# The final normalisation of an attention layer: scale and shift vectors in PSUM banks, epsilon on VectorE, a 512-column first centring piece

## The chip, the cores and the metric

One Trainium2 chip, one core. The metric is the device time of one execution in microseconds (us). The kernel before was timed in three runs. Engines are called as the profile calls them: PE is TensorE, DVE VectorE, ACT ScalarE, POOL GpSimd, and SP the engine whose queue issues most DMAs.

## The reference

One decoder layer on 512 rows of 2048 columns, float32 throughout: a differential attention with eight heads (each with two query and key parts of 128 columns and a value of 256), its output gated by silu(z), projected out and added to the scaled input; then a layer normalisation. What the change touches is the last line:

```
proj = x @ w_in                                   # q | k | v | z, 2048 x 8192
a    = softmax(q1 k1^T * s + bias) - lam * softmax(q2 k2^T * s + bias)
o    = rms_norm(a @ v, subln_g) * (1 - lam_init)
y    = (o * silu(z)) @ w_out                      # 2048 x 2048
r    = 2 ** 0.25 * x + y
out  = (r - mean(r)) * rsqrt(var(r) + 1e-5) * ln_g + ln_b
```

## The kernel before, in words

Each engine has its own program, written out by hand, and the engines meet at semaphores. Every float32 product is made of three fast ones: ACT rounds a weight or activation block to a high part, DVE subtracts that for a low part, and PE multiplies high by high, high by low and low by high.

The eight head pairs go through PE one after another (16 weight quarters each), then the out projection runs in four chunks of 512 columns (`c`), each over eight weight blocks (`i`). Chunks 0 and 2 are summed in the four PSUM banks `proj`, chunks 1 and 3 in the four banks `att`; bank `s` holds row tile `s` of 128 rows. Chunks 0 to 2 go through all four row tiles for each weight block. Chunk 3 goes tile by tile (PE's last loop, L931 to L939): tile `s` is finished with its 48 matmuls, and `tile_done` tells DVE, while PE goes on with the next. The banks `proj` are free from the moment that DVE has read chunk 2 (r_ready 12), and bank `s` of `att` from the moment that DVE has read tile `s` of chunk 3.

For tile `s` of chunk 3, the work is this.

- DVE adds the residual (L724: x_res times alpha, from SBUF, plus the PSUM bank), takes the statistics of 512 columns (L727) and aggregates those of all four chunks into mean and variance (L754).
- POOL adds epsilon to the variance (L379) and raises it to the power -1/2 (L382), which gives `r_std`.
- DVE centres the first 1024 columns, (r - mean) * ln_g, in one instruction (L759), waits for `r_std`, makes shift = -mean * r_std (L763), centres the next 512 columns (L759), then scales by `r_std` and adds ln_b on both pieces (L768). `VECTOR_PIECES` (L951) lists the two.
- ACT normalises the last 512 columns as r * r_std + shift (L541), and POOL multiplies them by ln_g (L387) and adds ln_b (L389). `POOL_PIECE` (L952) is that slice.
- SP stores the three pieces in the order in which they are written here (L328 twice, L330), each when it is ready, and waits at the end for all stores.

ln_g and ln_b lie as 128 x 2048 rows in SBUF, in `scratch` (L108), loaded during chunk 1 (L323, L324). `big` holds the rows r (`r_rows`). ACT's last other work before this stage is the weight splits of chunk 3 (L527), made ahead during chunk 2, and the load of the residual's input (`load_res`, L253, issued on ACT's queue).

Of the kernel before, what the change touches and what calls it, by code (L numbers as in the profile page):

```python
# [33 lines left out]
ALU = mybir.AluOpType  # L34
ACT = mybir.ActivationFunctionType
# [5 lines left out]
D = 2048  # L41
# [3 lines left out]
ST = SEQ // P  # L45
# [10 lines left out]
NC = 512  # L56
CHUNKS = D // NC
# [8 lines left out]
EPS = 1e-5  # L66
# [4 lines left out]
def diff_layer(nc, x, rel_bias, w_in, lam_q1, lam_k1, lam_q2, lam_k2, subln_g, w_out, ln_g, ln_b,  # L71
               x_cols, out):
    with ExitStack() as ctx:  # L73
# [3 lines left out]
        def sem(name):  # L77
            return ctx.enter_context(nc.semaphore(name))
# [29 lines left out]
        ln_g_all, ln_b_all = scratch[:, 0:D], scratch[:, D:2 * D]  # L108
# [22 lines left out]
        mean_var = sb("mean_var", [P, ST, 2])  # L131
        var_eps = sb("var_eps", [P, ST])
# [9 lines left out]
        turned = att[:, 2]  # L142
        av = att[:, 3, 0:PW]

        x_loaded = [sem(f"x_loaded{i}") for i in range(len(X_UNITS))]
        raw_loaded = [sem(f"raw_loaded{i}") for i in range(RING)]
        small_loaded = sem("small_loaded")
# [6 lines left out]
        ln_loaded = sem("ln_loaded")  # L154
# [51 lines left out]
        pool_scaled = sem("pool_scaled")  # L206
        pool_rows_ready = sem("pool_rows_ready")
        centred = sem("centred")
        rows_ready = sem("rows_ready")

        TOTAL = PAIRS * QUARTERS
# [39 lines left out]
        def load_res(eng, c):  # L251

            eng.dma_start(x_res[:], x[0, :, c * NC:(c + 1) * NC].rearrange("(s p) d -> p s d", p=P)  # L253
                          ).then_inc(res_loaded, 16)
# [80 lines left out]
        @block.gpsimd  # L335
        def _(pool):
            nc.gpsimd.memset(ident[:], 0.0).then_inc(ident_zero, 1)
            pool.wait_ge(ident_zero, 1)
            nc.gpsimd.affine_select(out=ident[:], in_=ident[:], compare_op=ALU.not_equal, fill=1.0, base=0,
                                    pattern=[[-1, P]], channel_multiplier=1).then_inc(consts_ready, 1)  # L340
            nc.gpsimd.memset(minus_half[:], -0.5).then_inc(consts_ready, 1)

            def spread_bias(p):

                heads = slice(2 * p, 2 * p + 2)
                pool.dma_start(bias_dram.ap()[heads].rearrange("h q w -> q h w"),
                               line_dram.ap()[heads].unsqueeze(0).to_broadcast([P, 2, BIAS_W])).then_inc(bias_spread, 16)

            nc.gpsimd.memset(bias_line[:, SEQ:BIAS_W], MASKED).then_inc(bias_line_ready, 1)
            pool.wait_ge(table_loaded, 16)  # L350
            for bucket, cols in BUCKET_RUNS:
                nc.gpsimd.tensor_copy(bias_line[:, cols],
                                      table[:, bucket:bucket + 1].to_broadcast([16, cols.stop - cols.start])
                                      ).then_inc(bias_line_ready, 1)
            pool.wait_ge(bias_line_ready, len(BUCKET_RUNS) + 1)
            pool.dma_start(line_dram.ap(), bias_line).then_inc(line_stored, 16)
            pool.wait_ge(line_stored, 16)
            spread_bias(0)
            pool.wait_ge(consts_ready, 2)
            for p in range(PAIRS):  # L360
                pool.wait_ge(bias_spread, 16 * (p + 1))
                if p:
                    pool.wait_ge(max_ready, 2 * ST * p)

                pool.dma_start(bias[:], bass.AP(bias_dram, 2 * p * P * BIAS_W + P - 1,
                                                [[BIAS_W - 1, P], [P * BIAS_W, 2], [1, SEQ]])).then_inc(bias_loaded, 16)
                if p + 1 < PAIRS:
                    spread_bias(p + 1)
                for t in range(ST):
                    n = ST * p + t + 1  # L370
                    pool.wait_ge(sq_ready, n)
                    nc.gpsimd.tensor_scalar(mean_sq[:, t:t + 1], sq_sum[:, t:t + 1], 1.0 / PW, EPS,  # L372
                                            ALU.mult, ALU.add).then_inc(mean_ready, 1)
                    pool.wait_ge(mean_ready, n)
                    nc.gpsimd.tensor_tensor(rms[:, t:t + 1], mean_sq[:, t:t + 1], minus_half[:],  # L375
                                            ALU.pow).then_inc(rms_ready, 1)
            for s in range(ST):
                pool.wait_ge(mv_ready, s + 1)
                nc.gpsimd.tensor_scalar(var_eps[:, s:s + 1], mean_var[:, s, 1:2], 1.0, EPS,  # L379
                                        ALU.mult, ALU.add).then_inc(var_ready, 1)  # L380
                pool.wait_ge(var_ready, s + 1)
                nc.gpsimd.tensor_tensor(r_std[:, s:s + 1], var_eps[:, s:s + 1], minus_half[:],  # L382
                                        ALU.pow).then_inc(r_std_ready, 1)

                part = r_rows[:, s, POOL_PIECE]
                pool.wait_ge(act_normed, s + 1)
                nc.gpsimd.tensor_tensor(part, part, ln_g_all[:, POOL_PIECE], ALU.mult).then_inc(pool_scaled, 1)  # L387
                pool.wait_ge(pool_scaled, s + 1)
                nc.gpsimd.tensor_tensor(part, part, ln_b_all[:, POOL_PIECE], ALU.add).then_inc(pool_rows_ready, 1)  # L389
# [3 lines left out]
        def _(act):  # L393
# [123 lines left out]
            for c in range(CHUNKS):  # L517
                for i in range(OQ):
                    if c == 0 and i in G_STEPS:
                        g_split_hi(G_STEPS[i])  # L520
                    for n in out_splits(c, i):
                        act.wait_ge(raw_loaded[ring(n)], 16 * (n // RING + 1))
                        if n < LAST:
                            act.wait_ge(quarter_done, n - LEAD)
                        elif n >= LAST + RING:
                            act.wait_ge(quarter_done, n - LEAD - RING)
                        nc.scalar.activation(out_split_view(n, 0), w_raw[:, ring(n)], ACT.Copy).then_inc(w_hi, 1)  # L527
                    if c == 0:
                        late_steps(PAIRS - 1, i)
                    if i == OQ - 2:  # L530
                        if c == 0:
                            for n in G_REST:
                                g_split_hi(n)
                            act.wait_ge(silu_ready, PAIRS * ST)
                        else:
                            act.wait_ge(r_ready, ST * c)
                        load_res(act, c)
            for s in range(ST):
                act.wait_ge(shift_ready, s + 1)
                part = r_rows[:, s, POOL_PIECE]  # L540
                nc.scalar.activation(part, part, ACT.Identity, scale=r_std[:, s:s + 1],  # L541
                                     bias=shift[:, s:s + 1]).then_inc(act_normed, 1)
# [3 lines left out]
        def _(dve):  # L546
# [202 lines left out]
            for s in range(ST):  # L749
                c = CHUNKS - 1  # L750
                dve.wait_ge(tile_done, s + 1)
                residual(c, s)
                dve.wait_ge(stats_ready, ST * c + s + 1)
                nc.vector.bn_aggr(mean_var[:, s], stats[:, s].rearrange("p c k -> p (c k)")).then_inc(mv_ready, 1)  # L754
                dve.wait_ge(mv_ready, s + 1)
                if s == 0:
                    dve.wait_ge(ln_loaded, 32)
                for cols in VECTOR_PIECES:
                    nc.vector.scalar_tensor_tensor(r_rows[:, s, cols], r_rows[:, s, cols], mean_var[:, s, 0:1],  # L759
                                                   ln_g_all[:, cols], ALU.subtract, ALU.mult).then_inc(centred, 1)  # L760
                    if cols == VECTOR_PIECES[0]:
                        dve.wait_ge(r_std_ready, s + 1)
                        nc.vector.scalar_tensor_tensor(shift[:, s:s + 1], mean_var[:, s, 0:1], -1.0,  # L763
                                                       r_std[:, s:s + 1], ALU.mult, ALU.mult
                                                       ).then_inc(shift_ready, 1)
                for i, cols in enumerate(VECTOR_PIECES):
                    dve.wait_ge(centred, len(VECTOR_PIECES) * s + i + 1)
                    nc.vector.scalar_tensor_tensor(r_rows[:, s, cols], r_rows[:, s, cols], r_std[:, s:s + 1],  # L768
                                                   ln_b_all[:, cols], ALU.mult, ALU.add).then_inc(rows_ready, 1)


        @block.tensor
# [175 lines left out]
G_ORDER = [*G_STEPS.values(), *G_REST]  # L948


VECTOR_PIECES = [slice(0, D // 2), slice(D // 2, 3 * D // 4)]  # L951
POOL_PIECE = slice(3 * D // 4, D)  # L952


# [37 lines left out]
```

## Time and profile before

| | |
|---|---|
| median of 3 runs | 983.01 us |
| lowest and highest run | 980.42 and 983.22 us |
| the profiled execution's own time | 980.93 us |
| its span in the profile | 979.1 us |
| PE busy | 963.7 us, 98% of the span |
| DVE, ACT, POOL busy | 448.8, 310.3 and 70.6 us |
| granted TensorE clock, mean | 0.995 |
| chain that ended last | PE 97%, DMA 1%, ACT 1%, all others 0% |

Busy times of the engines overlap, so they don't add up to the span. The chain that ended last is followed back from the last instruction, at each step to what released it. The profiled execution is 1.83 us longer than its span, which begins with the first and ends with the last recorded event.

### The profile page before, as it was taken

How to read it: one execution, taken by the hardware profiler on the slowest of the kernel's cores; microseconds unless marked ns; L12 is line 12 of the kernel's file. 1: busy time of each engine (PE TensorE's matmuls, PEld its weight loads, DVE VectorE, ACT ScalarE, POOL GpSimd, SP SyncE). 2: the span in 40 equal slices, each digit the busy share in tenths (PEclk: the TensorE clock that was granted, in tenths of full speed). 3: DMA queues.
4: the chain of work that ended last, by engine and by line, in shares of the span. 5: the costliest groups of instructions: out<-in, count | busy, mean ns of one | idle time of the engine just before them, and what ended most of it. 6: DMA issues, size and time to landing. Idle time of an engine off the chain costs nothing.

```text
span 979.1 us, 13373 instructions
## 1 busy us (share of the span) xinstructions
PE 963.7 (98%) x5200; PEld 835.8 (85%) x5200; DVE 448.8 (46%) x692; ACT 310.3 (32%) x491; POOL 70.6 (7%) x137
## 2 busy tenths in 40 slices
PE   8999999999999999999999999999999999999995
PEld 7898889888988898889888988898889888888884
DVE  4434533453345334533453345334533475425465
ACT  5324322432233224322432243224322463112200
POOL 2200100010001000100010001000100010000044
PEclk9999999999999999999999999999999999999998
DMA  9732422242224322432233224322332224442432
GB/s 306 254 87 87 134 87 86 87 132 87 86 86 131 89 86 86 129 90 86 86 128 92 86 86 126 94 86 86 97 95 86 86 70 142 175 151 86 151 115 101
DMA packets 85494, 108.63 MB, mean 111 GB/s; under 512 B 4176, under 2 KB 70224, under 8 KB 85216
## 3 DMA queue, kind: packets, MB, share of 16 engines
q1 hardware_dynamic: 81024, 94.65, 31.4%
q0 software_dynamic: 2336, 9.48, 2.8%
q10 hardware_dynamic: 2112, 4.19, 1.2%
q8 instruction: 15, 0.25, 0.1%
q14 instruction: 7, 0.06, 0.0%
HBM read 104.07 MB, written 9.48 MB: 116 GB/s over the span
## 4 chain that ended last, share of the span: by engine, by line
PE 97%; DMA 1%; ACT 1%; POOL 0%; DVE 0%; issue 0%; SPq 0%; POOLq 0%; ACTq 0%
PE proj L775 81%; PE att L775 15%; PE att L844 1%; PE att L869 1%; DMA big<-x_cols_dram 1%; POOL big L387 0%; POOLq L73 0%; POOL var_eps L379 0%; DVE xg_split L557 0%; ACT x_res L421 0%; ACT xg_split L404 0%; ACT w_split L527 0%; ACT scratch L419 0%; SPq L269 0%; ACT big L541 0%
## 5 line engine op out<-in xcount | busy, mean ns | idle before, releaser
L775 PE MATMUL proj<-xg_split,w_split 128*128 128x512 f32 x2304 | 539.9, 392 | 2.0 <-DVE w_split L673 2.0
L775 PEld LDWEIGHTS proj<-xg_split,w_split 128*128 128x128 f32 x2304 | 428.2, 188 | 89.5 <-DVE xg_split L557 2.4
L551 DVE TENSOR_TENSOR w_split<-w_raw,w_split 128x1024 fp32r<-128x1024 f32 x128 | 156.8, 1225 | 282.1 <-ACT w_split L400 281.5
L400 ACT ACTIVATE w_split<-w_raw 128x1024 fp32r<-128x1024 f32 x128 | 135.6, 1059 | 444.8 <-PE proj L775 435.7
L775 PE MATMUL proj<-w_split,xg_split 128*128 128x256 f32 (+1 forms) x1872 | 265.3, 302 | 0.0
L775 PEld LDWEIGHTS proj<-w_split,xg_split 128*128 128x128 f32 x1872 | 249.4, 191 | 13.5
L593 DVE CUSTOM_DVE_ANT_0 scratch<-att,bias 128x128 f32<-128x128 f32 (+3 forms) x64 | 28.9, 489 | 108.5 <-PE att L775 108.5
L775 PE MATMUL att<-operands 128*128 128x256 f32 (+2 forms) x432 | 71.1, 303 | 0.0
L775 PE MATMUL att<-w_split,xg_split 128*128 128x512 f32 x288 | 66.1, 389 | 0.0
L775 PEld LDWEIGHTS att<-operands 128*128 128x128 f32 x432 | 61.5, 190 | 3.1
L775 PEld LDWEIGHTS att<-w_split,xg_split 128*128 128x128 f32 x288 | 54.1, 188 | 11.2
L735 DVE TENSOR_TENSOR w_split<-w_raw,w_split 128x1024 fp32r<-128x1024 f32 x25 | 30.6, 1225 | 66.3 <-ACT w_split L527 66.3
L372 POOL TENSOR_SCALAR mean_sq<-sq_sum 128x1 f32<-128x1 f32 x32 | 8.4, 263 | 719.8 <-ACT scratch L443 719.8
L580 DVE RECIPROCAL scratch<-scratch 128x256 f32<-128x256 f32 x32 | 55.9, 1747 | 0.3
L527 ACT ACTIVATE w_split<-w_raw 128x1024 fp32r<-128x1024 f32 x25 | 26.5, 1060 | 87.9 <-PE proj L775 51.4
L428 ACT ACTIVATE scratch<-scratch,neg_max 128x128 f32<-128x128 f32 (+3 forms) x64 | 35.5, 556 | 32.5 <-DVE neg_max L598 32.5
L446 ACT ACTIVATE scratch<-att,o_scale 128x256 f32<-128x256 f32 x32 | 15.2, 475 | 39.8 <-DVE o_scale L625 39.8
L775 PE MATMUL att<-operands,xg_split 128*128 128x512 f32 x96 | 22.4, 389 | 0.0
L775 PEld LDWEIGHTS att<-operands,xg_split 128*128 128x128 f32 x96 | 18.0, 188 | 3.7
L614 DVE SCALAR_TENSOR_TENSOR scratch<-scratch,mix 128x128 f32<-128x128 f32 (+3 forms) x32 | 17.6, 552 | 3.2
L375 POOL TENSOR_TENSOR rms<-mean_sq,minus_half 128x1 f32<-128x1 f32 x32 | 18.6, 580 | 2.7
L625 DVE TENSOR_TENSOR o_scale<-rms,inv_sum 128x1 f32<-128x1 f32 x32 | 5.1, 160 | 26.8 <-POOL rms L375 26.8
(73 smaller groups left out, 412.8 us busy)
## 6 DMA issues: line engine op xcount, KB each, us to landing
w_raw<-in_w_in_dram SPq DMA_DIRECT2D x127, 512.0 KB, 3.6
w_raw<-in_w_out_dram SPq DMA_DIRECT2D x32, 512.0 KB, 3.8
bias_by_distance<-bias_lines POOLq DMA_DIRECT2D x8, 640.0 KB, 6.2
bias<-bias_by_distance POOLq DMA_DIRECT2D x8, 512.0 KB, 4.7
x_res<-in_x_dram ACTq DMA_DIRECT2D x4, 1024.0 KB, 5.1
big<-x_cols_dram SPq DMA_DIRECT2D x7, 512.0 KB, 8.0
out_dram<-big SPq DMA_DIRECT2D x4, 512.0 KB, 2.7
out_dram<-big SPq DMA_DIRECT2D x8, 256.0 KB, 2.5
```

Of the source, the lines that this page charges most:

```text
L375: nc.gpsimd.tensor_tensor(rms[:, t:t + 1], mean_sq[:, t:t + 1], minus_half[:], ALU.pow).then_inc(rms_ready, 1)
L400: nc.scalar.activation(split_view(a, 0), w_raw[:, ring(a)], ACT.Copy).then_inc(w_hi, 1)
L428: nc.scalar.activation(e, e, ACT.Exp, bias=neg_max[:, h:h + 1], accum_out=row_sum[:, h:h + 1]).then_inc(exp_ready, 1)
L446: nc.scalar.activation(normed[:, t], av, ACT.Copy, scale=o_scale[:, t:t + 1]).then_inc(normed_ready, 1)
L527: nc.scalar.activation(out_split_view(n, 0), w_raw[:, ring(n)], ACT.Copy).then_inc(w_hi, 1)
L551: nc.vector.tensor_tensor(split_view(a, 1), w_raw[:, ring(a)], split_view(a, 0).bitcast(F32), ALU.subtract).then_inc(w_ready, 1)
L580: nc.vector.reciprocal(part, part).then_inc(z_inv, 1)
L593: nc.vector.tensor_tensor_reduce(out=logits[:, h, 0:(t + 1) * P], in0=scores[:, h, 0:(t + 1) * P], in1=bias[:, h, (ST - 1 - t) * P:SEQ], s ...
L614: nc.vector.scalar_tensor_tensor(a_rows[:, t % 2, cols], logits[:, 1, cols], mix[:], logits[:, 0, cols], ALU.mult, ALU.add).then_inc(a_rea ...
L735: nc.vector.tensor_tensor(out_split_view(n, 1), w_raw[:, ring(n)], out_split_view(n, 0).bitcast(F32), ALU.subtract).then_inc(w_ready, 1)
L775: return nc.tensor.matmul(dst, lhsT, rhs, start=start, stop=stop, skip_group_check=True)
L844: last = nc.tensor.transpose(turned[:, cols], a_rows[:, t % 2, cols], ident[:])
```

## The change

ACT copies ln_g into the four banks `proj` once chunk 2 has been read, and, ahead of its pass of tile 3, the first 1536 columns of ln_b into banks 0 to 2 of `att`. DVE's centring reads ln_g from PSUM in all four tiles; its scaling and shifting reads ln_b from PSUM in tile 3 alone, and from SBUF in tiles 0 to 2. POOL's passes read both from SBUF as before. Epsilon is added by DVE, behind the aggregate. The centring goes in pieces of 512 and 1024 columns, the scaling and shifting in three of 512, and there are three stores of 512 columns ahead of POOL's.

```diff
+        g_banks, b_banks = proj, att
+        def bank_cols(banks, cols):
+            return banks[:, cols.start // NC:cols.stop // NC].rearrange("p b n -> p (b n)")
...
             for s in range(ST):
-                pool.wait_ge(mv_ready, s + 1)
-                nc.gpsimd.tensor_scalar(var_eps[:, s:s + 1], mean_var[:, s, 1:2], 1.0, EPS,
-                                        ALU.mult, ALU.add).then_inc(var_ready, 1)
                 pool.wait_ge(var_ready, s + 1)
...
                         load_res(act, c)
+            act.wait_ge(ln_loaded, 32)
+            act.wait_ge(r_ready, (CHUNKS - 1) * ST)
+            for c in range(CHUNKS):
+                last = nc.scalar.activation(g_banks[:, c], ln_g_all[:, c * NC:(c + 1) * NC], ACT.Copy)
+            last.then_inc(ln_moved, 1)
             for s in range(ST):
+                if s == ST - 1:
+                    act.wait_ge(r_ready, CHUNKS * ST - 1)
+                    for c in range(CHUNKS - 1):
+                        last = nc.scalar.activation(b_banks[:, c], ln_b_all[:, c * NC:(c + 1) * NC], ACT.Copy)
+                    last.then_inc(ln_moved, 1)
                 act.wait_ge(shift_ready, s + 1)
...
                 dve.wait_ge(mv_ready, s + 1)
+                nc.vector.tensor_scalar(var_eps[:, s:s + 1], mean_var[:, s, 1:2], EPS, None, ALU.add
+                                        ).then_inc(var_ready, 1)
                 if s == 0:
                     dve.wait_ge(ln_loaded, 32)
-                for cols in VECTOR_PIECES:
+                    dve.wait_ge(ln_moved, 1)
+                if s == ST - 1:
+                    dve.wait_ge(ln_moved, 2)
+                for cols in CENTRE_PIECES:
                     nc.vector.scalar_tensor_tensor(r_rows[:, s, cols], r_rows[:, s, cols], mean_var[:, s, 0:1],
-                                                   ln_g_all[:, cols], ALU.subtract, ALU.mult).then_inc(centred, 1)
-                    if cols == VECTOR_PIECES[0]:
+                                                   bank_cols(g_banks, cols), ALU.subtract, ALU.mult
+                                                   ).then_inc(centred, 1)
+                    if cols == CENTRE_PIECES[0]:
...
                 for i, cols in enumerate(VECTOR_PIECES):
-                    dve.wait_ge(centred, len(VECTOR_PIECES) * s + i + 1)
+                    dve.wait_ge(centred, len(CENTRE_PIECES) * s + min(i, 1) + 1)
                     nc.vector.scalar_tensor_tensor(r_rows[:, s, cols], r_rows[:, s, cols], r_std[:, s:s + 1],
-                                                   ln_b_all[:, cols], ALU.mult, ALU.add).then_inc(rows_ready, 1)
+                                                   bank_cols(b_banks, cols) if s == ST - 1 else ln_b_all[:, cols],
+                                                   ALU.mult, ALU.add).then_inc(rows_ready, 1)
...
-VECTOR_PIECES = [slice(0, D // 2), slice(D // 2, 3 * D // 4)]
+CENTRE_PIECES = [slice(0, NC), slice(NC, 3 * NC)]
+VECTOR_PIECES = [slice(c * NC, (c + 1) * NC) for c in range(CHUNKS - 1)]
```

DVE's instructions for the last row tile, in its program's order (the names left of the arrow are written, those right of it read; waits name the semaphores). Before:

```order
L754 BN_AGGR mean_var<-stats 128x2 [waits stats_ready]
L759 SCALAR_TENSOR_TENSOR big<-big,mean_var,scratch 128x1024 [waits mv_ready]
L763 SCALAR_TENSOR_TENSOR shift<-mean_var,r_std 128x1 [waits r_std_ready]
L759 SCALAR_TENSOR_TENSOR big<-big,mean_var,scratch 128x512
L768 SCALAR_TENSOR_TENSOR big<-big,r_std,scratch 128x1024 [waits centred]
L768 SCALAR_TENSOR_TENSOR big<-big,r_std,scratch 128x512 [waits centred]
```

and with the change, where the lines have other numbers (L770 adds epsilon, L778 centres, L783 makes the shift, L788 scales and shifts):

```order
L768 BN_AGGR mean_var<-stats 128x2 [waits stats_ready]
L770 TENSOR_SCALAR var_eps<-mean_var 128x1 [waits mv_ready]
L778 SCALAR_TENSOR_TENSOR big<-big,mean_var,proj 128x512 [waits ln_moved]
L783 SCALAR_TENSOR_TENSOR shift<-mean_var,r_std 128x1 [waits r_std_ready]
L778 SCALAR_TENSOR_TENSOR big<-big,mean_var,proj 128x1024
L788 SCALAR_TENSOR_TENSOR big<-big,r_std,att 128x512 [waits centred] x3
```

One instruction has come in ahead of the centring, 512 columns less stand ahead of the shift, and no large instruction reads two tensors from SBUF.

ACT's instructions at the program's end, before:

```order
L527 ACTIVATE w_split<-w_raw 128x1024 [waits quarter_done,raw_loaded3]
L253 DMA x_res<-in_x_dram 128x4x512 [waits r_ready]
L541 ACTIVATE big<-big,shift,r_std 128x512 [waits shift_ready] x4
```

and with the change:

```order
L531 ACTIVATE w_split<-w_raw 128x1024 [waits quarter_done,raw_loaded3]
L260 DMA x_res<-in_x_dram 128x4x512 [waits r_ready]
L545 ACTIVATE proj<-scratch 128x512 [waits r_ready,ln_loaded]
L545 ACTIVATE proj<-scratch 128x512 x3
L555 ACTIVATE big<-big,shift,r_std 128x512 [waits shift_ready] x3
L551 ACTIVATE att<-scratch 128x512 [waits r_ready]
L551 ACTIVATE att<-scratch 128x512 x2
L555 ACTIVATE big<-big,shift,r_std 128x512 [waits shift_ready]
```

The seven copies stand behind the last load and between ACT's passes of tiles 2 and 3. The code of POOL loses its first instruction per tile.

## Rows read from the trace of the kernel before

**Rows 1.** The page: span, TensorE's busy time, chain that ended last.
```profile
span 979.1 us, 13373 instructions
...
PE 963.7 (98%) x5200; PEld 835.8 (85%) x5200; DVE 448.8 (46%) x692; ACT 310.3 (32%) x491; POOL 70.6 (7%) x137
...
PE 97%; DMA 1%; ACT 1%; POOL 0%; DVE 0%; issue 0%; SPq 0%; POOLq 0%; ACTq 0%
```

**Rows 2.** Timeline, last tile: start, duration (us), engine, line, operation, idle before.
```profile
961.98 5.60 PE L775 MATMUL att<-w_split,xg_split 128*128 128x512 f32 x24
...
969.07 0.26 DVE L754 BATCH_NORM_AGGREGATE mean_var<-stats 128x2 f32<-128x24 f32 x1
969.37 1.28 DVE L759 SCALAR_TENSOR_TENSOR big<-big,mean_var,scratch 128x1024 f32<-128x1024 f32 x1
969.42 1.28 POOL L379 TENSOR_SCALAR var_eps<-mean_var 128x1 f32<-128x1 f32 x1 [4.07 <-DVE mean_var L754]
970.79 0.55 POOL L382 TENSOR_TENSOR r_std<-var_eps,minus_half 128x1 f32<-128x1 f32 x1
971.37 0.16 DVE L763 SCALAR_TENSOR_TENSOR shift<-mean_var,r_std 128x1 f32<-128x1 f32 x1 [0.72 <-POOL r_std L382]
971.45 0.74 DVE L759 SCALAR_TENSOR_TENSOR big<-big,mean_var,scratch 128x512 f32<-128x512 f32 x1
971.57 0.81 ACT L541 ACTIVATE big<-big,shift,r_std 128x512 f32<-128x512 f32 x1 [10.06 <-DVE shift L763]
972.11 2.94 DVE L768 SCALAR_TENSOR_TENSOR big<-big,r_std,scratch 128x1024 f32<-128x1024 f32 x2
972.46 2.05 POOL L387 TENSOR_TENSOR big<-big,scratch 128x512 f32<-128x512 f32 x1 [1.12 <-ACT big L541]
...
974.59 1.59 POOL L389 TENSOR_TENSOR big<-big,scratch 128x512 f32<-128x512 f32 x1
976.20 0.33 SPq L330 DMA_DIRECT2D out_dram<-big  x1
```

**Rows 3.** Timeline, chunk 3 before the last tile: ACT's load, DVE's and ACT's passes.
```profile
931.05 0.37 ACTq L253 DMA_DIRECT2D x_res<-in_x_dram  x1
...
937.61 0.26 DVE L754 BATCH_NORM_AGGREGATE mean_var<-stats 128x2 f32<-128x24 f32 x1
...
956.74 0.69 DVE L724 SCALAR_TENSOR_TENSOR big<-x_res,att 128x512 f32<-128x512 f32 x1 [3.42 <-PE att L775]
...
960.69 0.82 ACT L541 ACTIVATE big<-big,shift,r_std 128x512 f32<-128x512 f32 x1 [10.06 <-DVE shift L763]
```

**Rows 4.** POOL's epsilon adds in the attention: duration ns min/median/max, starts.
```profile
L372 POOL TENSOR_SCALAR mean_sq<-sq_sum x32: 192/236/380, 92.5 to 798.6; 128x1 f32<-128x1 f32 x32
```

**Rows 5.** Groups by line and shape behind the last matmul: busy us, mean ns.
```profile
L768 DVE SCALAR_TENSOR_TENSOR big<-big,r_std,scratch 128x512 f32<-128x512 f32 x1 | 1.7, 1745 | 0.0
...
L759 DVE SCALAR_TENSOR_TENSOR big<-big,mean_var,scratch 128x512 f32<-128x512 f32 x1 | 0.7, 745 | 0.0
```

**Rows 6.** The same view of DVE over the whole span.
```profile
L724 DVE SCALAR_TENSOR_TENSOR big<-x_res,att 128x512 f32<-128x512 f32 x8 | 5.5, 684 | 13.5 <-PE att L775 9.1 <-DMA x_res<-in_x_dram 4.4
...
L699 DVE TENSOR_SCALAR neg_lam<-lam_diff 128x1 f32<-128x1 f32 x1 | 0.2, 153 | 0.0
```

**Rows 7.** SP's first issues (timeline); DMA share and GB/s of a window, last two columns.
```profile
0.75 0.38 SPq L264 DMA_DIRECT2D big<-x_cols_dram  x1
1.18 0.42 SPq L269 DMA_DIRECT2D w_raw<-in_w_in_dram  x1
...
974.50:975.00 0.50, 0.00 (x0) 0.00 (x0) 0.50 (x1) 0.00 (x0) 0.42 (x2) 0.50 1.00 410
```

**Rows 8.** Groups of ACT over the whole span: its only table load.
```profile
L404 ACT ACT_TABLE_LOAD x1 | 1.3, 1283 | 0.7 <-PEq L979 0.7
```

**Rows 9.** The chain that ended last, its last two entries: start, duration (us).
```profile
880.54 43.52 PE proj L775 x192
924.07 43.53 PE att L775 x192
```

More of the change, by code:

```diff
@@ L208, in diff_layer @@
         centred = sem("centred")
+        ln_moved = sem("ln_moved")
         rows_ready = sem("rows_ready")
```

## Prediction

> **What bounds the kernel now.** I read the page first: TensorE is busy for 98% of the span, and the chain that ended last lies on it for 97% [rows 1]. The reader is to see that nothing before TensorE's last matmul can be bought by the normalisation unless it delays TensorE. The timeline of the last 12 us comes next: the last matmul ends at 961.98 + 5.60 = 967.58, and the span at 979.1, so an exposed tail of 11.5 us is left, and the change lives in it [rows 2]. The same work of row tiles 0 to 2 runs beside the matmuls of the next tile, whose end releases DVE 10.88 us after the one before (956.74, 967.62) [rows 2, 3], and costs nothing.
>
> In the tail two strands start at the statistics (DVE's L754, done at 969.33) [rows 2]. **Strand P**: POOL adds epsilon (1.28) and takes the power (0.55), DVE makes the shift (0.16, from 971.37), ACT normalises the fourth piece (0.81, from 971.57), POOL multiplies (2.05, from 972.46) and adds (1.59, to 976.18), SP issues the store at 976.20, and the span ends 2.90 later. **Strand V**: DVE centres 1024 columns, idles 0.72, centres 512, and scales and shifts both, to about 975.06; its last store is issued before POOL's. Strand P ends last, by 1.1 us.
>
> Two of POOL's times are not its own work. The epsilon add on 128x1 took 1.28, whereas the like instruction elsewhere took 0.19 to 0.38 [rows 4]; here it starts at 969.42 and ends at 970.70, just behind DVE's 1024-wide pass (969.37 to 970.65) [rows 2]. Then DVE's 512-wide L768 took 1.745, against 0.745 for the same shape at L759 [rows 5]. Laid end to end: DVE's first L768 ends at 972.11 + 1.28 = 973.39 (its 1024 columns priced as L759's), POOL's multiply at 974.51, DVE's second at 975.06, POOL's add at 976.18. The differences are 1.12, 0.55, 1.12: the engines take turns, and a POOL pass alone is worth some 1.12. The DVE instructions concerned read two tensors from SBUF. The Trainium skill, SBUF — State Buffer, section "Who interferes with whom", says just this: a DVE instruction with two SBUF inputs and a GpSimd one that reads SBUF shut each other out for a whole instruction, and with one SBUF input they don't. These rows agree with its first half; none shows the second, which the change relies on.
>
> **The change, part by part.**
> 1. *Epsilon on DVE.* Removed: 1.28 of POOL and its start. Added: a 128x1 DVE instruction at 0.15 (L699's price) [rows 6], from 969.37 to 969.52. POOL started 0.09 behind its releaser [rows 2], so the power runs from 969.61 to 970.16.
> 2. *Smaller first centring piece, scale from PSUM.* DVE back to back starts an instruction some 0.08 before the end of the one ahead (L763 and L759 in [rows 2]). So the 512-wide piece starts at 969.44. Its price: L724, with in0 in SBUF and in1 in PSUM, takes 0.684; from SBUF alone L759 takes 0.745 [rows 5, 6]. I take 0.69, the nearer form; it ends at 970.13, just inside POOL's power, and the 0.03 to the shift puts that at 970.19, not 971.37. Gain 1.18. POOL's multiply then starts at 972.46 - 1.18 = 971.28. Bounds for the power: 0.55 if PSUM reads let it through, and 0.55 behind the end of the centring (970.68, gain only 0.66) if they hold it off.
> 3. *POOL's two passes.* Bounds 1.12 (taking turns is the whole excess) and the 2.05 and 1.59 of today. I take 1.12, since in the last tile DVE reads both scale and shift from PSUM: multiply to 972.40, 0.08 between, add 972.48 to 973.60. POOL is done 2.58 earlier than 976.18.
> 4. *DVE's own strand.* The second centring piece, 1024 wide, from 970.27 at 1.22 (1.28 less the 0.06 of PSUM) to 971.49, then three pieces at 0.69, overlapping by 0.08: ends 972.10, 972.71, 973.32.
> 5. *Stores.* SP now issues four of 256 KB in order, not 512, 256 and 256. Its issues stand 0.43 apart at the closest (0.75 to 1.18 [rows 7]), so POOL's goes behind the one of 973.34 at 973.77, not at 973.62: 0.15 lost. The DMA engines, when full, moved 410 GB/s [rows 7], 0.64 per 256 KB; stores issued at 972.12, 972.73, 973.34 and 973.77 leave the last one waiting 0.30. Bounds 0 and 0.4. Then 2.90 as before.
> 6. *Seven ACT copies of 128x512 into PSUM.* No row has ACT writing PSUM. The nearest is ACT's pass L541, as wide, SBUF to SBUF, at 0.81 [rows 2]; I price with that. Four of them stand behind the last x_res load (ACT, 931.05 [rows 3]), which waits for the last read of the `proj` banks as they do; at 0.81 they end by 934.7, and DVE wants them after tile 0's aggregate (937.61 [rows 3]). Nothing else is queued on ACT until tile 0's shift. The other three follow tile 2's ACT pass (960.69 + 0.82) and need banks 0 to 2 of `att`, free since the read of 956.74 [rows 3]; they end by 964.0, when DVE wants them after 971.4. Both are covered by TensorE's matmuls of the tiles in hand; without that cover they would cost up to 3.2 and 2.4. ACT already goes from Copy to Identity now, and has one table load in the whole run, its first [rows 8]. Cost 0; bounds 0 and the whole 5.7, if TensorE stood still beside them (a rival below).
> 7. *Tiles 0 to 2* still read the shift vector from SBUF; more turns there are hidden, since DVE is idle 3.42 before the next residual [rows 3].
>
> The sum: -2.58 + 0.15 + 0.30 = -2.13 us, hence 978.8 against the profiled execution's 980.93. That execution lies low in the runs shown (980.42 to 983.22); against their median of 983.01 the same step gives 980.9, my forecast. What a measurement of this kernel can tell from no change, 0.3%, is 2.95 us: more than the whole gain.
>
> A rule that speaks against the change: the Trainium skill, Perfetto Trace Analysis, on per-instruction access overhead, puts DVE at about 60 ns on SBUF and 125 ns on PSUM. By it the five DVE passes would each be longer by 0.065, DVE's end some 0.3 later, and the gain about 1.8. The trace disagrees: L724 at 0.684 is below L759 at 0.745 [rows 5, 6], and the measurement decides.
>
> **Rivals.**
> - *Forecast*: turns vanish, -2.1. For it: the three differences above. Chance 0.62.
> - *More than that*: the stores don't queue and POOL is under 1.12. DVE's last store, issued at 973.34, keeps this to at most 2.9, so -2.6 to -2.9: 978.0 to 978.3 on the profiled scale. Chance 0.08.
> - *POOL's passes stay slow*: POOL with 512 columns simply needs 1.6 each. For it: the add is at 1.59 though DVE shares only its first 0.5. Against it: that DVE's pass stretches by a whole 1.0. Then only 1.18 + 0.44 = 1.6 goes, or 1.2 if the multiply stays at 2.05: 979.3 to 979.7, by the median 981.4 to 981.8. Chance 0.15.
> - *DVE becomes the bound through slower PSUM reads*: 0.81 and 1.35 in place of 0.69 and 1.22 (the 0.06 with the other sign). Then DVE ends at 973.88, SP issues POOL's store at 974.33, 0.2 of queueing: -1.65, 979.3, by the median 981.4. L724 in rows 6 is against it. The Trainium skill, Perfetto Trace Analysis, is for it. Chance 0.08.
> - *The power is still held off*, and with it the passes: -0.66 or less, 980.3 to 980.9; by the median 982.4 to 983.0. Chance 0.03.
> - *Slower*: ACT's writes into PSUM hold up TensorE's, in other banks of the same memory. Place: 931 to 935 and 961.5 to 964. Price: 7 x 0.81 = 5.7 stalled at most, less 2.1: +3.6, 984.5, by the median 986.6. It decides from 2.1 of stall on, and counts as slower by over 0.3% from 5.1. Against it: DVE's PSUM reads beside TensorE leave a chunk of 192 matmuls at 43.52 and 43.53 [rows 9]; these are reads, so it isn't excluded. Chance 0.04.
>
> **How the numbers follow.** The likeliest case gives 980.9. The range goes from 980.42 - 2.6 = 977.8 (lowest run shown, with the second case) to 983.2 (highest run, gain near 0); the runs' own spread of 2.8 makes most of it, and the slower case is left out. Faster by over 0.3% needs 2.95: within the forecast, scatter of the runs could show it in about one of four (0.15), in the second case in four of ten (0.03): 0.18. Slower 0.04, within 0.3% 0.78.
>
> **What would show it.** In the timeline behind the last matmul: the power 0.55 long and beginning about 2.0 behind it; the shift at 2.6 behind it (3.8 now); POOL's multiply and add near 1.1 each; DVE passes of 512 at 0.69, all within 5.75 of the matmul; SP's last issue at 6.2 (8.6 now) and the end at some 9.4 (11.5 now). A multiply at 1.6 or more with DVE on PSUM operands refutes step 3; 0.80 for a DVE pass refutes step 2; any matmul group over 43.6 speaks for the slower case. A store that lands over 3.2 behind its issue would show step 5 too small. The prediction is wrong if the tail is shorter than 8.5 or longer than 11.

## The result, and the profile after

| | before | with the change |
|---|---|---|
| median of 22 runs | 982.72 us | 981.27 us |
| lowest and highest | 980.42 and 983.29 | 979.34 and 982.62 |
| the profiled execution, time / span | 980.93 / 979.1 | 981.34 / 979.5 |
| end of the last matmul in it | 967.58 | 969.67 |
| from there to the end of the span (tail) | 11.52 | 9.83 |

The ratio of the times is 0.9986, 95% interval 0.998 to 0.9993: a gain of 0.7 to 2.0 us, clear of the noise and below 0.3%. The two profiled executions differ by more than the change does, and the other way: the changed kernel's last matmul ends 2.09 later. That comes from the opening, which the change doesn't touch (last section). What the change does is read from the tail, which came out 0.02 apart in two profiles of the changed kernel: 9.83 here, 9.85 in the second. The profile prints spans to 0.1 us, so a tail, and a time from issue to end, is good to some 0.05.

The timeline of the changed kernel behind its last matmul (start, duration in us, engine, line, operation, idle before) answers to [rows 2]:

```profile
964.07 5.60 PE L796 MATMUL att<-w_split,xg_split 128*128 128x512 f32 x24
...
971.16 0.26 DVE L768 BATCH_NORM_AGGREGATE mean_var<-stats 128x2 f32<-128x24 f32 x1
971.46 0.15 DVE L770 TENSOR_SCALAR var_eps<-mean_var 128x1 f32<-128x1 f32 x1
971.53 0.74 DVE L778 SCALAR_TENSOR_TENSOR big<-big,mean_var,proj 128x512 f32<-128x512 f32 x1
971.69 0.55 POOL L386 TENSOR_TENSOR r_std<-var_eps,minus_half 128x1 f32<-128x1 f32 x1 [6.22 <-DVE var_eps L770]
972.27 0.16 DVE L783 SCALAR_TENSOR_TENSOR shift<-mean_var,r_std 128x1 f32<-128x1 f32 x1
972.35 1.27 DVE L778 SCALAR_TENSOR_TENSOR big<-big,mean_var,proj 128x1024 f32<-128x1024 f32 x1
972.47 0.81 ACT L555 ACTIVATE big<-big,shift,r_std 128x512 f32<-128x512 f32 x1 [8.54 <-DVE shift L783]
973.36 1.26 POOL L391 TENSOR_TENSOR big<-big,scratch 128x512 f32<-128x512 f32 x1 [1.12 <-ACT big L555]
973.54 2.06 DVE L788 SCALAR_TENSOR_TENSOR big<-big,r_std,att 128x512 f32<-128x512 f32 x3
974.31 1.65 SPq L335 DMA_DIRECT2D out_dram<-big  x3
974.70 1.27 POOL L393 TENSOR_TENSOR big<-big,scratch 128x512 f32<-128x512 f32 x1
976.00 0.45 SPq L337 DMA_DIRECT2D out_dram<-big  x1
```

Counted from the last matmul's end (969.67), the power starts at 2.02, the shift at 2.60, POOL's multiply at 3.69, its add is done at 6.30, SP issues the last store at 6.33, and the span ends at 9.83. Before, the shift came at 3.79 and the last issue at 8.62. So 2.29 was won up to the last issue, and 0.60 given back behind it: 3.50 from issue to end, in place of 2.90.

The groups of the same stretch, one row for each shape (busy us, mean ns | idle before), answer to [rows 5]:

```profile
L788 DVE SCALAR_TENSOR_TENSOR big<-big,r_std,att 128x512 f32<-128x512 f32 x3 | 2.1, 742 | 0.0
L778 DVE SCALAR_TENSOR_TENSOR big<-big,mean_var,proj 128x1024 f32<-128x1024 f32 x1 | 1.3, 1274 | 0.0
L393 POOL TENSOR_TENSOR big<-big,scratch 128x512 f32<-128x512 f32 x1 | 1.3, 1266 | 0.1
L391 POOL TENSOR_TENSOR big<-big,scratch 128x512 f32<-128x512 f32 x1 | 1.3, 1265 | 1.1 <-ACT big L555 1.1
```

No DVE pass is stretched any more (0.742 where it was 1.745), and POOL's two passes take 1.265 and 1.266 in place of 2.05 and 1.59. In tiles 0 to 2, where DVE still reads ln_b from SBUF, its three passes take 4.03 and POOL's add 1.61, in the same program (tile 2):

```profile
962.66 4.03 DVE L788 SCALAR_TENSOR_TENSOR big<-big,r_std,scratch 128x512 f32<-128x512 f32 x3
...
963.86 1.61 POOL L393 TENSOR_TENSOR big<-big,scratch 128x512 f32<-128x512 f32 x1
```

Against the rival that ended on the slower side stand the chain's last chunk and the copies (groups of ACT; the row of the chain gives start and duration):

```profile
926.15 43.53 PE att L796 x192
```

```profile
L545 ACT ACTIVATE proj<-scratch 128x512 f32<-128x512 f32 x4 | 2.2, 588 | 6.3 <-DVE big L738 6.3
L551 ACT ACTIVATE att<-scratch 128x512 f32<-128x512 f32 x3 | 1.6, 582 | 0.0
```

All seven copies run inside that chunk, which takes 43.53 as before [rows 9]. Here ACT's writes to free banks cost TensorE nothing, and ACT's 0.59 a copy was hidden.

### The profile page after: what moved, and what is told of

It reads as the page before. It is cut to its first block, busy times and chain, and to the rows that moved or that the text cites. A ratio compares the mean times of both kernels' runs of the same rounds, so it can differ in the third digit from the quotient of the medians.

```text
span 979.5 us, 13389 instructions
## 1 busy us (share of the span) xinstructions
PE 964.3 (98%) x5200; PEld 835.9 (85%) x5200; DVE 451.6 (46%) x700; ACT 314.2 (32%) x498; POOL 62.0 (6%) x133
## 4 chain that ended last, share of the span: by engine, by line
PE 97%; DMA 1%; ACT 1%; DVE 0%; issue 0%; SPq 0%; POOLq 0%; POOL 0%; ACTq 0%
PE proj L796 81%; PE att L796 15%; PE att L865 1%; PE att L890 1%; DMA big<-x_cols_dram 1%; POOLq L73 0%; POOL big L391 0%; DVE xg_split L571 0%; ACT x_res L425 0%; ACT xg_split L408 0%; ACT w_split L531 0%; ACT scratch L423 0%; SPq L276 0%; ACT big L555 0%; SPq L271 0%
## 5 line engine op out<-in xcount | busy, mean ns | idle before, releaser
L796 PEld LDWEIGHTS att<-w_split,xg_split 128*128 128x128 f32 x288 | 54.1, 188 | 11.2
```

What stands on the lines that cost most here:

```text
L796: return nc.tensor.matmul(dst, lhsT, rhs, start=start, stop=stop, skip_group_check=True)
```

## The experiments

Every kernel has a profile, and the parts of the change are told apart by its tail. Whole times are compared where a kernel was run several times, always with the kernel before on the same chip.

**e1_eps_alone: one part alone.** The kernel before, with

```diff
-                pool.wait_ge(mv_ready, s + 1)
-                nc.gpsimd.tensor_scalar(var_eps[:, s:s + 1], mean_var[:, s, 1:2], 1.0, EPS,
-                                        ALU.mult, ALU.add).then_inc(var_ready, 1)
...
                 dve.wait_ge(mv_ready, s + 1)
+                nc.vector.tensor_scalar(var_eps[:, s:s + 1], mean_var[:, s, 1:2], EPS, None, ALU.add
+                                        ).then_inc(var_ready, 1)
```

> The kernel before with one part of the change: DVE adds epsilon (128x1) and POOL only takes the power; the first centring piece is 1024 columns, all vectors in SBUF. All times from the end of the last matmul. Theory (turns): POOL's power, issued at 2.0, is shut out by the 1024-column centring pass that reads two SBUF tensors (1.86 to 3.14), so it shows over 1.1 long instead of 0.55 and the shift comes at 3.2 to 3.6 (3.79 before): a gain of 0.2 to 0.6 in the tail, which was 11.5. Rival (the epsilon add simply took 1.28 on POOL): the power is 0.55 long and the shift waits for DVE's own centring, at 3.1.

Timeline of this kernel, whose last matmul ends at 967.12:

```profile
968.98 1.27 DVE L758 SCALAR_TENSOR_TENSOR big<-big,mean_var,scratch 128x1024 f32<-128x1024 f32 x1
969.14 1.52 POOL L379 TENSOR_TENSOR r_std<-var_eps,minus_half 128x1 f32<-128x1 f32 x1 [4.46 <-DVE var_eps L753]
970.70 0.16 DVE L762 SCALAR_TENSOR_TENSOR shift<-mean_var,r_std 128x1 f32<-128x1 f32 x1 [0.44 <-POOL r_std L379]
```

The power, 0.55 long elsewhere, takes 1.52 and ends 0.41 behind DVE's pass. The shift comes at 3.58, the tail is 11.28: a gain of 0.24. The epsilon add had not been slow; it had waited, and the power took over its wait. Moved by itself, it brings 0.24. The range expected for the shift, 3.2 to 3.6, was met.

**e2_no_psum: everything but PSUM.** The changed kernel without the copies; DVE reads `ln_g_all[:, cols]` and `ln_b_all[:, cols]` throughout.

> The changed kernel without any copy to PSUM: both vectors are read from SBUF; epsilon on DVE, the small first centring piece, the three 512-column passes and four stores are kept. Theory (turns): the power is held off by the 512-column centring pass and is over 0.55 long, POOL's multiply and add are near 2 and 1.6 instead of 1.27, DVE's three last passes take 4 in all instead of 2.06, and the tail is 11.2 to 12, as long as before or longer: 1.4 to 2.1 us above the changed kernel. Rival (order and epsilon did it, PSUM is worth nothing): tail 9.8, the same time as the changed kernel.

Its timeline, last matmul at 966.93:

```profile
968.79 0.74 DVE L765 SCALAR_TENSOR_TENSOR big<-big,mean_var,scratch 128x512 f32<-128x512 f32 x1
968.95 0.99 POOL L386 TENSOR_TENSOR r_std<-var_eps,minus_half 128x1 f32<-128x1 f32 x1 [5.67 <-DVE var_eps L760]
...
971.06 1.39 POOL L391 TENSOR_TENSOR big<-big,scratch 128x512 f32<-128x512 f32 x1 [1.12 <-ACT big L545]
971.25 4.08 DVE L775 SCALAR_TENSOR_TENSOR big<-big,r_std,scratch 128x512 f32<-128x512 f32 x3
...
975.73 0.46 SPq L337 DMA_DIRECT2D out_dram<-big  x1
```

Tail 12.27, 0.75 more than before the change; time 1.0009 of the kernel before (1.0 to 1.0019). The power again ends 0.41 behind the pass that held it off. POOL's multiply is then ready while the second centring pass still runs, so POOL steps in twice, behind that pass and behind the first scaling pass, and each time DVE's next pass is stretched to 1.75: 4.08 for work that takes 2.06. DVE is done only at 8.40, behind POOL (7.19), and the last store waits for DVE's on SP until 8.80. The theory held, but the expectation missed in two places. The multiply took 1.39, not 2, as it only met the last 0.27 of the second centring pass. And the tail came out longer than the 11.2 to 12 expected: it is 2.44 above the changed kernel's, not 1.4 to 2.1.

**e3_shift_in_sbuf: the last tile's ln_b from SBUF.**

```diff
-                if s == ST - 1:
-                    act.wait_ge(r_ready, CHUNKS * ST - 1)
...
-                                                   bank_cols(b_banks, cols) if s == ST - 1 else ln_b_all[:, cols],
+                                                   ln_b_all[:, cols],
```

> The changed kernel without the three copies of ln_b: the last tile reads ln_b from SBUF as tiles 0 to 2 do, ln_g from PSUM. Theory (turns): the last tile looks like tiles 0 to 2 of the changed kernel: the shift at 2.6 from the last matmul, POOL's multiply 1.3, its add 1.6, DVE's three last passes 4.0 in all, so that DVE and not POOL ends last, at 7.9, and the tail is 11.2 to 11.8: 1.4 to 2.0 us above the changed kernel. Rival (only the scale vector's move matters): tail under 10.2, time the same within 0.4.

Its timeline, last matmul at 969.59:

```profile
973.27 1.26 POOL L391 TENSOR_TENSOR big<-big,scratch 128x512 f32<-128x512 f32 x1 [1.12 <-ACT big L550]
973.45 3.96 DVE L781 SCALAR_TENSOR_TENSOR big<-big,r_std,scratch 128x512 f32<-128x512 f32 x3
974.62 1.59 POOL L393 TENSOR_TENSOR big<-big,scratch 128x512 f32<-128x512 f32 x1
...
977.82 0.46 SPq L337 DMA_DIRECT2D out_dram<-big  x1
```

DVE now ends last, at 7.82, and POOL's finished rows wait behind its stores on SP until 8.23. Tail 11.71; time 1.0001 of the kernel before (0.9992 to 1.001). With the scale vector alone in PSUM the change would have moved nothing that can be measured in the whole time. On top of all the rest, the three ln_b copies are worth 1.88 of the tail. The other half, ln_b in PSUM and ln_g in SBUF, was not tried.

**e4_alpha_column: why a PSUM pass took 0.74 and not 0.69.**

```diff
+            nc.gpsimd.memset(alpha[:], ALPHA).then_inc(consts_ready, 1)
...
-                nc.vector.scalar_tensor_tensor(r_rows[:, s, c * NC:(c + 1) * NC], x_res[:, s], ALPHA,
+                nc.vector.scalar_tensor_tensor(r_rows[:, s, c * NC:(c + 1) * NC], x_res[:, s], alpha[:],
```

> The changed kernel with the residual's factor read from a 128x1 column instead of standing in the instruction as a constant, all else the same. It asks why DVE's passes with a PSUM operand took 0.74 and not the 0.69 of the residual pass. Theory: a pass that reads its factor from a column costs some 0.05 more than one with a constant, wherever the other operands lie: the residual goes from 0.687 to 0.73 to 0.75. Rival (it is which operand lies in PSUM, or what PE does meanwhile): the residual stays at 0.687.

The residual's group in this kernel, over the whole span:

```profile
L742 DVE SCALAR_TENSOR_TENSOR big<-x_res,alpha,att 128x512 f32<-128x512 f32 x8 | 5.9, 744 | 11.9 <-PE att L800 7.4 <-DMA x_res<-in_x_dram 4.5
```

0.744, against 0.684 with the constant [rows 6]. The 0.06 belongs to the factor that is read from a column, not to where the tensor lies.

**Behind the last issue: what makes the last store slow.** Four kernels ask what the store waits for. In three only stores are left out; e8 also makes ACT wait for POOL in every tile, which moves the ln_b copies 3.6 later, still ahead of the last matmul.

*e6_two_stores_less* leaves out the last tile's stores of columns 0 to 1023.

> The changed kernel that leaves out two stores of the last tile (its columns 0 to 1023 never reach DRAM); the stores of columns 1024 to 1535 and of POOL's piece go out at 5.95 and 6.33 as before. Theory (queueing of four): with two, the last waits some 0.3 behind the other: 3.1 to 3.2 from issue to end, tail 9.45. Rival (the distance of 0.38 to the store ahead on SP's queue does it): 3.5, tail 9.83. If neither matters, 2.9 and 9.2.

Measured: 3.32 from issue to end, tail 9.72, between the theory's range and the rival. The queue's share had been put too small for a store that follows 0.38 behind another.

*e9_pool_store_alone* leaves out all three stores ahead of POOL's, *e10_third_store_less* only the third (`if s < ST - 1 or cols != VECTOR_PIECES[-1]`).

> The changed kernel that leaves out the three stores of the last tile's columns 0 to 1535, so that POOL's store at 6.33 is alone. Theory (queueing behind the row stores): 2.8 to 2.95 from issue to the end, as before the change, tail 9.2. Rival (a store that late, or PE's stop, makes it slow anyway): 3.3 or more.

> The changed kernel that leaves out one store of the last tile, that of columns 1024 to 1535; those of 4.64 and 5.27 stay, POOL's goes out at 6.33. With the first two left out instead, the last store took 3.32. Theory (what counts is how many bytes are still ahead when it is issued): the two stores are through by 6.8, so nearly nothing is ahead of data that begins at 7.2: 2.9 to 3.0, tail 9.25. Rival (every earlier store costs its share, 0.2 each): 3.2 to 3.3.

SP's last issue in the first (last matmul 967.36, span 976.6) and in the second (969.18, 978.4):

```profile
973.75 0.33 SPq L338 DMA_DIRECT2D out_dram<-big  x1
```

```profile
975.56 0.33 SPq L338 DMA_DIRECT2D out_dram<-big  x1
```

2.85 and 2.84 from issue to end, tails 9.24 and 9.22; the last issue comes at 6.39 and 6.38. The two early stores alone cost nothing; the third, issued 0.38 ahead of the last, costs 0.47 from issue to end alone (e6) and 0.65 with the two before it. By the tails it is 0.48 and 0.6, as the changed kernel issues its last store 0.06 earlier.

*e8_store_on_act* issues POOL's store from ACT's queue (`act.wait_ge(pool_rows_ready, s + 1)`, `act.dma_start(...)`).

> The changed kernel with POOL's store issued from ACT's queue instead of SP's, so that it has no issue just ahead of it on its queue; same moment, 6.3 from the last matmul. Theory (the DMA engines are busy with the three stores ahead): still 3.4 to 3.5 from its issue to the end of the span, tail 9.8. Rival (SP's queue delays an issue that follows 0.38 behind another): 2.9 to 3.1, tail 9.3.

Its last store (last matmul 967.87, span 977.8):

```profile
974.21 0.34 ACTq L555 DMA_DIRECT2D out_dram<-big  x1
```

Issued at 6.34, done 3.59 later, tail 9.93, against the 2.9 to 3.1 of the rival: the queue it comes from doesn't matter. That leaves the DMA engines. Their windows in the changed kernel, last store's issue (976.00) included (the last two columns are their busy share and GB/s):

```profile
975.50:976.00 0.50, 0.00 (x0) 0.00 (x0) 0.10 (x1) 0.00 (x0) 0.47 (x1) 0.50 1.01 369
976.00:976.50 0.50, 0.00 (x0) 0.00 (x0) 0.00 (x0) 0.00 (x0) 0.00 (x0) 0.50 1.05 324
976.50:977.00 0.50, 0.00 (x0) 0.00 (x0) 0.00 (x0) 0.00 (x0) 0.00 (x0) 0.50 1.18 311
977.00:977.50 0.50, 0.00 (x0) 0.00 (x0) 0.00 (x0) 0.00 (x0) 0.00 (x0) 0.50 1.01 340
```

Their busy share is 1.0 or more, and they move 311 to 369 GB/s, not the 410 of the wide store before [rows 7]; e9's store, alone, moved up to 393. An estimate from these rows fits: at 340 GB/s a store of 256 KB takes 0.77, so three that start one behind another from 4.64 keep the last, issued at 6.33, waiting for 0.62; 0.60 more than before was measured. The same count, on top of the 2.9 of a store that waits for none, gives 3.3 for e6, 2.9 for e10 and, below, 3.4 for e7 and 3.9 for e5 (its wide store at 410 GB/s): all within 0.1 of what came.

**e5_wide_store and e7_first_piece_early: stores and order.** e5 joins the first two stores of a tile (1024 columns, sent when both passes are done); e7 has DVE scale and store its first piece ahead of the second centring pass.

> The changed kernel with its first two stores per tile joined into one of 1024 columns, issued when both passes are done: three stores of 512, 256 and 256 KB as before the change, the last two issued at 5.95 and 6.33. Theory (queueing by bytes): data can only begin at some 6.0 instead of 5.35, rows of 4 KB move at some 400 GB/s instead of 310, so the last store is done at about the same moment or slightly later: 3.3 to 3.7 behind its issue, tail 9.7 to 10.0. Rival (what delays the last store is the count of 2 KB rows): 2.9 to 3.1, tail 9.3.

> The changed kernel with DVE's order altered: the first 512 columns are scaled and shifted straight behind the shift vector, ahead of the centring of the other 1024, so that their store goes out at 3.4 from the last matmul instead of 4.64. DVE's work and POOL's are the same. Theory (the four stores queue at the DMA engines, and that is why the last one took 3.5 from issue to the end of the span instead of 2.9): only the last two stores still overlap, the last takes 3.1 to 3.25, and the tail is 9.4 to 9.6 instead of 9.83. Rival (a store close behind another on SP's queue, or one of 2 KB rows, simply lands later): 3.5 again, tail 9.83. In either case the time is below the kernel before by 1.5 to 2.2.

e5: last issue at 6.33, 4.01 to the end, tail 10.34, worse than the theory or the rival said. Waiting 0.65 longer for a wider store leaves more bytes ahead of the last one. e7: tail 9.96, not 9.4 to 9.6; last issue 6.46, 3.50 to the end; time 0.9985 of before (0.9976 to 0.9994), as the changed kernel's. One store went early, but the second of four was issued only at 5.4, and DVE ended 0.13 later, since its last two passes waited for the wide centring pass. The count of what still overlaps was wrong in the expectation: it must be made to the last byte ahead, not by stores.

**after_again and e11_piece_by_piece: a faster version.** The changed kernel once more, with 12 runs, and a kernel in which DVE goes piece by piece:

```diff
+                for cols in VECTOR_PIECES:
+                    i = VECTOR_PIECES.index(cols)
+                    nc.vector.scalar_tensor_tensor(r_rows[:, s, cols], r_rows[:, s, cols], mean_var[:, s, 0:1],
+                                                   bank_cols(g_banks, cols), ALU.subtract, ALU.mult
+                                                   ).then_inc(centred, 1)
...
+                    dve.wait_ge(centred, len(VECTOR_PIECES) * s + i + 1)
...
+                sp.wait_ge(rows_ready, len(VECTOR_PIECES) * s + 3)
+                sp.wait_ge(pool_rows_ready, s + 1)
+                sp.dma_start(out[0, s * P:(s + 1) * P, 2 * NC:], r_rows[:, s, 2 * NC:]).then_inc(out_stored, 16)
```

The first two pieces are stored alone, columns 1024 to 2047 together.

> The changed kernel unaltered, for comparison on the same chip: tail 9.8 within 0.1, last store 3.5 from issue to the end of the span; time 1.0 to 1.9 below the kernel before.

> A try at a faster version: DVE goes piece by piece (centre 512, shift vector, scale 512; then centre and scale each of the next two), with stores of columns 0 to 511 at 3.45 and 512 to 1023 at 4.85, and one of columns 1024 to 2047 (4 KB rows) when DVE and POOL are both done, at 6.35. Expected by the queue theory: the first two are through before the last begins, and 512 KB at 400 GB/s takes 0.65 more than 256 KB alone, so 3.3 to 3.6 from issue to end and a tail of 9.6 to 9.9, that is within 0.25 of the changed kernel; time 1.4 to 1.9 below the kernel before. If DVE ends after 6.35 because of the waits between dependent passes, the store is that much later.

after_again: 0.9987 of before (0.9978 to 0.9996), tail 9.85. e11: 0.9976 (0.9964 to 0.9988), median 978.98 of 7 runs against 981.55 of 11 before on the same chip; tail 9.40, better than expected. Its timeline, last matmul at 967.50:

```profile
970.95 1.77 SPq L336 DMA_DIRECT2D out_dram<-big  x2
...
972.54 1.27 POOL L394 TENSOR_TENSOR big<-big,scratch 128x512 f32<-128x512 f32 x1
973.06 0.75 DVE L789 SCALAR_TENSOR_TENSOR big<-big,r_std,att 128x512 f32<-128x512 f32 x1
973.88 0.33 SPq L339 DMA_DIRECT2D out_dram<-big  x1
```

DVE and POOL end together, at 6.31; by the same count two stores are through before the last is issued at 6.38, and the span ends 3.02 later, though this store has 512 KB, in rows of 4 KB. The 3.3 to 3.6 expected priced the second 256 KB by bytes, at 0.65; it cost 0.17 more than e9's single 256 KB. The page of the kernel before had the price (KB each, median us from issue to landing):

```profile
out_dram<-big SPq DMA_DIRECT2D x4, 512.0 KB, 2.7
out_dram<-big SPq DMA_DIRECT2D x8, 256.0 KB, 2.5
```

Why a store of twice the bytes lands only 0.2 later, while a second store close ahead costs 0.47, was not tried. The tail is 0.43 shorter than the changed kernel's; how much of that is DVE's order and how much the joined store was not told apart, but e7's order and e5's joined store gained nothing by themselves. The intervals of the two ratios overlap, so that it beats the changed kernel rests on the tails; that it beats the kernel before is measured.

## Why the prediction was right, and what in it was not

The sign, the bound (within 0.3%) and the mechanism were right, and the gain was put too large: -2.13 was forecast, -1.69 came in the tail and -1.45 between the medians, and the interval of the ratio allows 2.0 at most. That 981.27 lies as near to the forecast 980.9 is in part luck: the forecast started from 983.01, the median of three runs, and the median of 22 is 982.72, so a base 0.29 too high took away some of the error.

Nor does the time single out the forecast. Two rivals, POOL's passes at 1.6 and DVE's at 0.81, had been priced at 981.4 and at -1.6 and -1.65, nearer to what came. Only the trace parts them: POOL's passes took 1.265 and DVE's 0.742. Point by point, by the prediction's steps:

1. *Epsilon on DVE*: 0.15, and the power starts at 2.02, as worked out. That the add's 1.28 had been a wait is shown by e1.
2. *The shift* at 2.60; forecast 2.61. The first centring piece is just hidden behind the power, as said, though at 0.736 and not 0.69: it had been priced by L724, whose factor is a constant. e4 shows that this makes the 0.06. The bound left open, the power held off by DVE, was decided by PSUM: 0.55 with it, 0.99 in e2. The Trainium skill's rule in "Who interferes with whom" (SBUF — State Buffer) that a DVE instruction with one SBUF input leaves GpSimd alone now has its rows too: 0.55 for the power beside L778, 1.265 for POOL's multiply beside it. The figures of the Trainium skill, Perfetto Trace Analysis, "Optimizing Scalar/DVE Operations", for DVE's access overhead (about 125 ns on PSUM against 60 on SBUF) don't show here, where one operand still lies in SBUF: like for like, 0.736 to 0.742 with a PSUM operand and 0.745 without.
3. *POOL's passes*: the mechanism was right, and the size too small by 0.14 each: 1.265, not 1.12. Laying the blocked passes end to end gives only what is left of a pass once it is let in; the other 0.14 had fallen into its wait. For the two passes, +0.29 on the sum.
4. *DVE's strand* ended at 5.93 instead of 5.74, by the 0.05 of each pass; it isn't the one that ends last.
5. *Stores*: the 0.15 for SP's queue didn't arise, as it took the next issue 0.37 behind the last. The wait at the DMA engines was mis-sized the other way: 0.60 measured, 0.30 forecast (its own figures add up to 0.27), and the last store's 3.50 is past the 3.2 that the prediction named as the sign of it. 410 GB/s had been taken for stores that move 311 to 369 when they overlap. Together +0.15.
6. *ACT's copies*: free, at 0.59 each; the slower rival is out, by the chunk of 43.53.
7. *Tiles 0 to 2*: hidden, with 3.02 of DVE's idle time left before the next residual.

The sum of the errors, 0.29 - 0.15 + 0.30 = 0.44, is the difference between 2.13 and 1.69, as far as spans printed to 0.1 can tell. So two terms were mis-sized: POOL's pass in step 3 and the queue at the DMA engines in step 5.

What none of the steps had said is how the parts hang together. By tails: 11.52 before, 11.28 with epsilon moved, 12.27 with the small pieces and four stores as well, 11.71 with ln_g in PSUM, 9.83 with ln_b too. In this order the steps give 0.24, lose 0.99, give 0.56 and give 1.88: until the last is in, the tail is at best 0.24 shorter than before. Other orders were not run. Nor was the old division into pieces with both vectors in PSUM, so what the small pieces and the fourth store are worth in the changed kernel isn't known.

## What to carry to other kernels

Where DVE and POOL work side by side and DVE reads two tensors from SBUF, look for instructions that are longer than their like elsewhere: they may be waiting for each other, and moving one of them can hand the wait to the next, as in e1. Copying the constant operand to a free PSUM bank took the wait away here, but it paid only once it was done for the last passes that meet POOL too (e3 against the changed kernel). In a tail that ends with stores, count the bytes of other stores still ahead of the last one when it is issued, and let them go early or with it (e11).

## What the runs showed of the hardware that was not expected

**The opening sets two levels of time.** In the 14 executions profiled here the last matmul ended either between 966.5 and 967.9 (nine) or between 969.2 and 970.1 (five), whatever the kernel. The runs of the result fall into two groups as well: 9 of the kernel before from 980.4 to 981.9 and 13 from 982.4 to 983.3, 8 of the changed kernel from 979.3 to 980.2 and 14 from 981.2 to 982.6. Within each group the medians differ by some 1.5, which agrees with the tails. The windows of 10 to 15 us tell them apart (the third column from the end is the granted TensorE clock), first the kernel before, then the changed one:

```profile
5.00:10.00 5.00, 4.18 (x14) 2.85 (x13) 2.00 (x4) 2.51 (x4) 0.00 (x0) 1.00 1.01 349
10.00:15.00 5.00, 3.85 (x17) 3.21 (x18) 4.59 (x5) 3.92 (x4) 0.00 (x0) 1.00 1.06 383
```

```profile
5.00:10.00 5.00, 3.32 (x13) 2.10 (x12) 1.59 (x4) 2.33 (x4) 0.00 (x0) 1.00 0.93 304
10.00:15.00 5.00, 3.21 (x8) 2.56 (x9) 4.52 (x5) 3.49 (x5) 0.00 (x0) 0.66 1.07 386
```

In the second TensorE was busy for 3.32 of the 5 us before, not 4.18, and then its clock was granted at 0.66 on the mean (part of the time at 1.2 in place of 2.4 GHz): 8 matmuls in place of 17 in that window. after_again, e3 and e10 show the 0.66 as well, and e4 0.82 there and 0.84 in the 5 us behind it; the other nine executions show 1.00. By the chain that ended last, TensorE's next 276 matmuls took 54.06 from 11.79, against 52.60 from 11.15 before: 0.64 and 1.46, together the 2.1 by which the changed kernel's profiled execution was behind when its tail began. The clock is what parts the two levels: those 276 matmuls took 54.05 to 54.19 in the five late executions and 52.56 to 52.60 in the other nine. A late start doesn't: e10 began them at 11.17 and is late, e8 at 11.51 and is not. What makes the clock fall isn't shown. Little work just before isn't enough for it: TensorE was busy for only 3.37 and 3.43 of the 5 us in e1 and e7 and kept the full clock, and for 3.94 in e4, which lost part of it. Nor was it tried why the first loads arrive later in some executions.

**A POOL instruction that is held off needs 0.14 less than alone once it is let in.** From the end of DVE's pass the power needed 0.41 more (0.55 alone), in both e1 and e2, and the 128x512 multiply of e2 needed 1.12 more (1.265 alone). That some start-up of it runs during the wait would explain this; it wasn't tested.
